# The opening of a four-layer forward pass on one core: constants and vectors issued by SyncE behind the weights, the first weight unit in two transfers, the first piece split ahead of the first squares

## The chip, the cores and the metric

The kernel runs on one core of a Trainium2 chip. The metric is the device time in microseconds of one execution, the median of several. Before the change it is 3043.73 us (three runs, 3043.11 to 3044.73).

## What is computed

Two blocks of two layers each on x of 512 positions by 1024 channels, float32. The first block alternates an even layer (dilated attention beside a short gated convolution) and an odd layer (chunkwise retention), each followed by a gated feed-forward part with a causal depthwise convolution. The second block has two layers of sparse attention (compressed, selected and window branches) beside stick-breaking attention, and the same kind of feed-forward part. Only the beginning of the first layer matters here:

```python
y = xf * lax.rsqrt(jnp.mean(xf * xf, axis=-1, keepdims=True) + EPS)
xn = (y * g.astype(jnp.float32)).astype(x.dtype)
proj = xn @ w_in                        # 1024 -> 1536 + 1536
q, k, v, gate_b, gate_c, h = jnp.split(proj, ...)
q = rms_norm(heads(q), q_gain)
```

## The kernel before, in words

**Layout.** x is held with channels on partitions: eight tiles of 128 channels by 512 positions. The kernel multiplies in float32 by splitting both operands into a rounded high part and the rest: `wh` and `wl` for weights, `xh` and `xl` for activations. Each product of a 128x128 weight column block with a 128x512 tile is three matmuls, wh*xh (L460), wl*xh (L463) and wh*xl (L467).

**Weights.** All weights come in *units* of 128 x 1024 floats (512 KB) into a ring of four slots. A unit has two *pieces* of 512 columns, a piece four blocks of 128. SyncE issues the units in order (`sync_program`, L422); unit u waits until both pieces of unit u-4 have been split. ScalarE makes the high part of each piece (`hi_to`, L973), VectorE the low part (`lo_to`, L1346), and both have four piece buffers: the split of piece i waits until TensorE has used piece i-4. The order is written out by hand: each engine's program says at which points pieces are split, up to three pieces ahead of TensorE.

**The opening.** SyncE issues tile 0 of x and then units 0 to 3. ScalarE issues the eight columns of `vec` that hold the first gains, then the other seven tiles of x in four transfers (L1077), then the rest of `vec`, the constants `cst`, the positions and the mask of the dilated attention (L1079 to L1082), then loads its activation table (L1083). The first norm is taken out of the product: x times the gain goes into TensorE, and the result is later multiplied by the root of the mean square of each position (`rs`). So for each tile j ScalarE makes `xh` (`prescale`, L980) and the square (L984), VectorE `xl` (L1354) and the running sum of squares (L1363). This is `first_tile`. Three output tiles are made at once in the first group: TensorE takes k = 0 to 7 and for each k the next three weight blocks, first the high and low weight of each against `xh(k)`, then the three against `xl(k)`. Piece 0 therefore serves k = 0 and one block of k = 1, piece 1 the rest of k = 1 and two blocks of k = 2.

The driver on ScalarE and VectorE is `group(..., ahead=1)`: `first_tile(0)`, then for each k `first_tile(k + 1)` and the splits up to piece (3(k + 1) - 1) // 4 + 3. On ScalarE the order before is thus: xh0, square 0, xh1, square 1, pieces 0 to 3, xh2, square 2, piece 4 (waits for TensorE), xh3 and so on.

**Who waits for the moved transfers.** The constants are first used by TensorE's column sums of the squares (L557) after the first group, the positions and the rest of `vec` by VectorE well behind that, and the mask by the attention.

**The end of the opening.** Pieces 0 to 5 belong to the first group, 6 and 7 to the next tile, 8 and 9 (unit 4) to the one after it.

Of the kernel before, what the change touches and what calls it, by code (L numbers as in the profile page):

```python
# [16 lines left out]
S = 512  # L17
# [5 lines left out]
RING = 4  # L23
UNIT = 1024
HALF = 512
# [9 lines left out]
NVEC = _at  # L35
# [3 lines left out]
for _name, _n in (("ident", 128), ("ones", 128), ("tri", 128), ("neg", 128), ("rot", 128), ("blk", 2), ("mhalf", 64),  # L39
# [3 lines left out]
NCST = _at  # L43

FLAGS = ("proj", "stat", "attn", "hi", "act", "lo", "dve", "pool", "land0", "land1", "land2", "land3",
         "x0", "x1", "x2", "x3", "x4", "gain", "cst", "vec", "pos", "dil", "ret", "out")


class Flag:
# [329 lines left out]
def build(nc, D, out):  # L379
    with ExitStack() as ctx:  # L380
        K = memory(nc, ctx)
        K.D, K.out, K.W = D, out, weights(D)
        for program in (sync_program, scalar_program, vector_program, gpsimd_program, tensor_program):
            program(Count(), Queue(None), K)
        for flag in K.F:
            flag.count = 0
        block = ctx.enter_context(nc.Block())

        @block.sync
        def _(e):  # L390
            sync_program(e, Queue(e), K)

        @block.scalar
        def _(e):
            scalar_program(e, Queue(e), K)

        @block.vector
        def _(e):
            vector_program(e, Queue(e), K)

        @block.gpsimd
        def _(e):
            gpsimd_program(e, Queue(e), K)

        @block.tensor
        def _(e):
            tensor_program(e, Queue(e), K)


def sync_program(e, q, K):  # L410

    F, W = K.F, K.W
    e.dma_start(K.x(0), K.D["x"][:, 0:S]).then_inc(F.x0.tell("x", by=16), 16)
    for u, (src, width, pieces) in enumerate(W.units):
        if u >= RING:
            before = W.units[u - RING][2]
            for p in before:
                q.wait_ge(F.hi, ("piece", p))
                q.wait_ge(F.lo, ("piece", p))
            if len(before) == 0:  # L420
                q.wait_ge(F.attn, ("unit", u - RING))
        e.dma_start(K.slot(u)[:, 0:width], src).then_inc(K.landed(u).tell(("unit", u), by=16), 16)  # L422
    for j in range(DT):
        if j in (1, 3, 5):
            q.wait_ge(F.pool, ("x", "end", j))
        else:
            q.wait_ge(F.dve, ("x", "end", j))
        e.dma_start(K.out[:, j * S:(j + 1) * S], K.x(j)).then_inc(F.out.tell(("out", j), by=16), 16)
    q.wait_ge(F.out, ("out", DT - 1))
    q.wait_ge(F.proj, ("tile", "down", 3, DT - 1))  # L430
# [529 lines left out]
def scalar_program(e, q, K):  # L960
    F, W, BK = K.F, K.W, K.BK
    nxt = [0]

    def hi_to(p):

        while nxt[0] <= min(p, len(W.pieces) - 1):
            i = nxt[0]
            nxt[0] += 1
            u, c, w = W.pieces[i]
            q.wait_ge(K.landed(u), ("unit", u))  # L970
            if i >= SPLIT:
                q.wait_ge(F.proj, ("piece", i - SPLIT))
            e.activation(K.wh(i, 0, w), K.raw(i), ACT.Copy, bias=0.0, scale=1.0).then_inc(F.hi.tell(("piece", i)), 1)  # L973

    def hi_for(key):
        hi_to(W.ahead(key))

    def prescale(s, j):

        e.activation(K.xh(j), K.x(j), ACT.Copy, bias=0.0, scale=K.vec(GAIN[s][0], GAIN[s][1] + j)).then_inc(  # L980
            F.act.tell(("xh", s, j)), 1)

    def square(s, j, src):
        e.activation(K.tmp(j % 3), src, ACT.Square, bias=0.0, scale=1.0).then_inc(F.act.tell(("sq", s, j)), 1)  # L984
# [5 lines left out]
    def group(key, n, feed, hooks={}, nk=DT, ahead=3):  # L990
        for k in range(ahead):
            feed(k)
        for k in range(nk):
            if ahead == 3:
                hi_to(W.first[key] + ((k + 1) * n - 1) // 4 + 3)
            if k + ahead < DT:
                feed(k + ahead)
            hi_to(W.first[key] + ((k + 1) * n - 1) // 4 + 3)
            if k in hooks:
                hooks[k]()  # L1000
# [66 lines left out]
    def first_tile(j):  # L1067
        q.wait_ge((F.x0, F.x1, F.x2, F.x2, F.x3, F.x3, F.x4, F.x4)[j], "x")
        q.wait_ge(F.gain, "gain")
        if j >= 3:  # L1070
            q.wait_ge(F.dve, ("sqa", s, j - 2))
        prescale(s, j)
        square(s, j, K.x(j))

    e.dma_start(K.VC[:, 0:8], K.D["vec"][:, 0:8]).then_inc(F.gain.tell("gain", by=16), 16)
    for i, (j0, j1) in enumerate(((1, 2), (2, 4), (4, 6), (6, 8))):
        e.dma_start(K.X[:, j0 * S:j1 * S], K.D["x"][:, j0 * S:j1 * S]).then_inc(  # L1077
            (F.x1, F.x2, F.x3, F.x4)[i].tell("x", by=16), 16)
    e.dma_start(K.VC[:, 8:NVEC], K.D["vec"][:, 8:NVEC]).then_inc(F.vec.tell("vec", by=16), 16)  # L1079
    e.dma_start(K.C[:, :], K.D["cst"]).then_inc(F.cst.tell("cst", by=16), 16)  # L1080
    e.dma_start(K.POSI, bass.AP(K.D["pos"].tensor, 0, [[0, 128], [1, S]])).then_inc(F.pos.tell("pos", by=16), 16)
    e.dma_start(K.DIL, K.D["dil"]).then_inc(F.dil.tell("dil", by=16), 16)  # L1082
    e.preload_act_table_set("natural_log_exp_and_others")  # L1083
    group(("e", "g"), 3, first_tile, ahead=1)
    hi_for(("e", 3))
    rs_row(s)
# [150 lines left out]
    for l in range(2):  # L1237
# [47 lines left out]
        for t in range(18):  # L1285
# [31 lines left out]
            if 0 <= t - 2 < 16 and (t - 2) % 4 == 3:  # L1317
                j = (t - 2) // 4
# [16 lines left out]
def vector_program(e, q, K):  # L1335
    F, W, BK = K.F, K.W, K.BK
    nxt = [0]

    def lo_to(p):

        while nxt[0] <= min(p, len(W.pieces) - 1):
            i = nxt[0]
            nxt[0] += 1
            w = W.pieces[i][2]
            q.wait_ge(F.hi, ("piece", i))
            e.tensor_tensor(K.wl(i, 0, w), K.raw(i), K.wh(i, 0, w).bitcast(F32), ALU.subtract).then_inc(  # L1346
                F.lo.tell(("piece", i)), 1)
# [4 lines left out]
    def prescale(s, j):  # L1352
        q.wait_ge(F.act, ("xh", s, j))
        e.scalar_tensor_tensor(out=K.xl(j), in0=K.x(j), scalar=K.vec(GAIN[s][0], GAIN[s][1] + j),  # L1354
                               in1=K.xh(j).bitcast(F32), op0=ALU.mult, op1=ALU.subtract).then_inc(
            F.dve.tell(("xl", s, j)), 1)

    def add_squares(s, j, final):

        q.wait_ge(F.act, ("sq", s, j))  # L1360
        if j > 1:
            q.wait_ge(F.dve, ("sqa", s, j - 1))
        e.tensor_tensor(K.tmp(j % 3), K.tmp(j % 3), K.tmp((j - 1) % 3), ALU.add).then_inc(  # L1363
            F.dve.tell(("sqa", s, j), *([("sq", s)] if j == final else [])), 1)
# [77 lines left out]
    s = ("e",)  # L1442

    def first_tile(j):
        prescale(s, j)
        if j:
            add_squares(s, j, DT - 1)

    def qk_tile(j):
# [3 lines left out]
        times_rs(K.Q[j], key, s, ("qkraw", j))  # L1453

    group(("e", "g"), 3, first_tile, ahead=1)
    late_norm(s, ("e", 3))
    for j in range(3):
# [307 lines left out]
    for l in range(2):  # L1765
# [119 lines left out]
        for t in range(18):  # L1885
            if t < 16:
                j, kt = t // 4, 3 - t % 4
# [295 lines left out]
```

## Time and profile before

| What | us |
|---|---|
| Median of three runs | 3043.73 (3043.11 to 3044.73) |
| The profiled execution's own time | 3045.64 |
| Its span, first to last instruction | 3043.9 |
| TensorE busy in the span | 3007.7 (99%) |
| VectorE busy | 1772.2 (58%) |
| ScalarE busy | 1267.3 (42%) |

The profile is of one execution, its times count from the span's start. PE is TensorE's matmuls, PEld its weight loads, DVE VectorE, ACT ScalarE, SP SyncE; a name with a q at the end (SPq, ACTq) is the engine's own issuing of DMAs. A matmul's duration in the timeline is longer than the distance to the next one, since matmuls overlap; in the chain in order of time each stands with the part in which it was the last. The granted clock of TensorE is given as a share of 2.4 GHz: 1.00 or 0.50.

### The profile page before, as it was taken

The numbers are of one execution on the slowest core, as the hardware profiler recorded it, in microseconds if no ns is written. First come the engines' busy times: TensorE is split into PE (matmuls) and PEld (weight loads), VectorE is DVE, ScalarE is ACT, GpSimd is POOL, SyncE is SP. The second block draws the span as 40 slices with busy tenths as digits, with TensorE's granted clock in tenths as the row PEclk, the third lists the DMA queues.
The fourth block names the chain that finished last, engine by engine and source line by source line (L and its number), as shares of the span: only waits on it lengthen the run. The fifth ranks groups of instructions, "written<-read, shape, count | busy, mean of one in ns | idle before, by whom it ended". The sixth has DMA issues, their size and how long they took to land.

```text
span 3043.9 us, 37845 instructions
## 1 busy us (share of the span) xinstructions
PE 3007.7 (99%) x14656; PEld 2403.0 (79%) x14656; DVE 1772.2 (58%) x3123; ACT 1267.3 (42%) x2374; POOL 146.3 (5%) x203
## 2 busy tenths in 40 slices
PE   8999999999999999999999999999999999999998
PEld 7678888888778888888866687888788766788886
DVE  4565875345554487634465567775364655577743
ACT  4344443323223344432366544443233655354431
POOL 0100000000000000001001101000020011010000
PEclk9899999999999999999999999999999999999999
DMA  3222323222222233332311132323232011223332
GB/s 143 75 87 95 100 97 97 97 89 76 82 78 84 90 104 97 97 97 92 102 38 42 42 98 81 100 97 97 90 99 91 29 49 46 93 84 104 97 97 69
DMA packets 71891, 260.35 MB, mean 86 GB/s; under 512 B 8096, under 2 KB 8096, under 8 KB 71584
## 3 DMA queue, kind: packets, MB, share of 16 engines
q1 hardware_dynamic: 70272, 252.67, 25.9%
q10 hardware_dynamic: 1440, 5.26, 0.4%
q8 instruction: 116, 1.90, 0.3%
q14 instruction: 63, 0.52, 0.1%
HBM read 255.81 MB, written 2.10 MB: 85 GB/s over the span
## 4 chain that ended last, share of the span: by engine, by line
PE 93%; DVE 4%; ACT 2%; issue 1%; ACTq 0%; POOL 0%; DVEq 0%
PE bank L460 25%; PE bank L463 24%; PE bank L467 24%; PE bank L537 2%; PE bank L541 2%; PE bank L538 2%; PE bank L617 2%; PE bank L649 2%; PE bank L631 1%; PE bank L773 1%; PE bank L890 1%; DVE wl L1346 1%; DVE big L1919 1%; PE bank L920 1%; ACT big L1325 1%
## 5 line engine op out<-in xcount | busy, mean ns | idle before, releaser
L1346 DVE TENSOR_TENSOR wl<-ring,wh 128x512 fp32r<-128x512 f32 (+1 forms) x944 | 646.8, 691 | 820.9 <-ACT wh L973 815.8
L460 PE MATMUL bank<-xh,wh 128*128 128x512 f32 x2464 | 989.0, 401 | 17.7 <-ACT wh L973 10.7
L463 PE MATMUL bank<-xh,wl 128*128 128x512 f32 x2464 | 966.9, 392 | 0.4 <-DVE wl L1346 0.3
L467 PE MATMUL bank<-xl,wh 128*128 128x512 f32 x2464 | 926.5, 391 | 0.0
L973 ACT ACTIVATE wh<-ring 128x512 fp32r<-128x512 f32 (+1 forms) x944 | 579.4, 622 | 810.5 <-PE bank L467 732.2
L460 PEld LDWEIGHTS bank<-xh,wh 128*128 128x128 f32 x2464 | 466.5, 189 | 152.8 <-issue 38.3
L467 PEld LDWEIGHTS bank<-xl,wh 128*128 128x128 f32 x2464 | 465.2, 189 | 99.7 <-DVE xl L1439 0.4
L463 PEld LDWEIGHTS bank<-xh,wl 128*128 128x128 f32 x2464 | 467.0, 190 | 92.0 <-DVE wl L1346 1.6
L460 PE MATMUL bank<-bigr,wh 128*128 128x512 f32 x1024 | 399.1, 390 | 0.6 <-ACT bigr L1329 0.6
L463 PE MATMUL bank<-bigr,wl 128*128 128x512 f32 x1024 | 398.5, 389 | 0.0
L467 PE MATMUL bank<-bigr,wh 128*128 128x512 f32 x1024 | 393.5, 389 | 0.0
L460 PEld LDWEIGHTS bank<-bigr,wh 128*128 128x128 f32 x1024 | 192.2, 188 | 41.4 <-ACT bigr L1329 1.4
L467 PEld LDWEIGHTS bank<-bigr,wh 128*128 128x128 f32 x1024 | 192.2, 188 | 40.6 <-DVE bigr L1923 0.9
L463 PEld LDWEIGHTS bank<-bigr,wl 128*128 128x128 f32 x1024 | 192.3, 188 | 39.6
L1142 ACT ACTIVATE tmp<-tmp,vec 128x512 f32<-128x512 f32 x136 | 104.7, 770 | 182.0 <-DVE tmp L1396 182.0
L1042 ACT ACTIVATE pp<-pp,sm 128x512 f32<-128x512 f32 (+3 forms) x160 | 88.3, 553 | 91.3 <-DVE sm L1415 91.1
L1152 ACT ACTIVATE bigr<-tmp 128x512 fp32r<-128x512 f32 x88 | 55.6, 632 | 138.3 <-DVE tmp L1591 138.3
L1396 DVE TENSOR_TENSOR big<-bank,rs 128x512 f32<-128x512 f32 x106 | 71.6, 687 | 69.1 <-PE bank L467 66.0
L1948 POOL TENSOR_TENSOR sm<-sm,cst 128x4 f32<-128x4 f32 x16 | 16.6, 1036 | 1952.6 <-DVE sm L1368 1618.5
L1396 DVE TENSOR_TENSOR tmp<-bank,rs 128x512 f32<-128x512 f32 x154 | 105.3, 684 | 6.9 <-ACT rs L988 4.3
L537 PE MATMUL bank<-wh,xh 128*128 128x512 f32 (+1 forms) x288 | 106.8, 371 | 0.0
L541 PE MATMUL bank<-wl,xh 128*128 128x512 f32 (+1 forms) x288 | 105.8, 367 | 0.0
(199 smaller groups left out, 2766.6 us busy)
## 6 DMA issues: line engine op xcount, KB each, us to landing
ring<-in_w_up SPq DMA_DIRECT2D x176, 512.0 KB, 3.4
ring<-in_w_down SPq DMA_DIRECT2D x88, 512.0 KB, 3.4
ring<-in_w_in SPq DMA_DIRECT2D x64, 512.0 KB, 3.5
ring<-in_w_ret SPq DMA_DIRECT2D x32, 512.0 KB, 3.2
ring<-in_w_even SPq DMA_DIRECT2D x20, 512.0 KB, 3.5
ring<-in_w_ret_v SPq DMA_DIRECT2D x16, 512.0 KB, 3.3
ring<-in_w_ret_out SPq DMA_DIRECT2D x16, 512.0 KB, 3.3
ring<-in_w_proj SPq DMA_DIRECT2D x16, 512.0 KB, 3.4
```

What stands on the lines that cost most here:

```text
L460: e.matmul(o, K.wh(p, c * 128, 128), oh, start=start, stop=False, skip_group_check=True)
L463: e.matmul(o, K.wl(p, c * 128, 128), oh, start=False, stop=False, skip_group_check=True)
L467: m = e.matmul(o, K.wh(p, c * 128, 128), ol, start=False, stop=stop, skip_group_check=True)
L537: e.matmul(o, K.XH[:, c], K.wh(p, 0, n), start=k == 0, stop=False)
L538: e.matmul(o, K.XL[:, c], K.wh(p, 0, n), start=False, stop=False)
L541: m = e.matmul(o, K.XH[:, c], K.wl(p, 0, n), start=False, stop=k == DT - 1)
L617: m = e.matmul(BK[i][:, u.at:u.at + w], u.q[r, u.qt * 128:w], u.k[r, 0:w], start=True, stop=True, skip_group_check=True)
L973: e.activation(K.wh(i, 0, w), K.raw(i), ACT.Copy, bias=0.0, scale=1.0).then_inc(F.hi.tell(("piece", i)), 1)
L1042: e.activation(p, p, ACT.Exp, bias=K.den(t, 2 * part + i, 0), scale=-1.0, accum_out=K.den(t, 2 * part + i, 1)).then_inc(F.act.tell(("exp", ...
L1142: e.activation(K.tmp((2 * i + 1) % 5), K.up(i), ACT.Identity, bias=b, scale=w[2]).then_inc(F.act.tell(("tap", f, i)), 1)
L1346: e.tensor_tensor(K.wl(i, 0, w), K.raw(i), K.wh(i, 0, w).bitcast(F32), ALU.subtract).then_inc(F.lo.tell(("piece", i)), 1)
L1396: e.tensor_tensor(dst, K.bank(key)[:, :], K.RSB[:, :], ALU.mult).then_inc(F.dve.tell(("freed", *key), *events), 1)
```

## The change

Three edits, all in the opening.

1. The four transfers of the rest of `vec`, `cst`, the positions and the mask leave ScalarE's program. SyncE issues them, right after unit 3 and ahead of unit 4.
2. Unit 0 comes in two transfers of 128 x 512 floats. The first tells a flag of its own, `first`, for which ScalarE's split of piece 0 waits; the second tells the unit's flag, for which piece 1 waits.
3. In `first_tile(0)` ScalarE splits piece 0 (high part) between xh0 and the square of tile 0, and VectorE splits it (low part) ahead of xl0.

```diff
--- before.py
+++ after.py
@@ -43,7 +43,7 @@
 NCST = _at
 
 FLAGS = ("proj", "stat", "attn", "hi", "act", "lo", "dve", "pool", "land0", "land1", "land2", "land3",
-         "x0", "x1", "x2", "x3", "x4", "gain", "cst", "vec", "pos", "dil", "ret", "out")
+         "x0", "first", "x1", "x2", "x3", "x4", "gain", "cst", "vec", "pos", "dil", "ret", "out")
 
 
 class Flag:
@@ -419,7 +419,16 @@
                 q.wait_ge(F.lo, ("piece", p))
             if len(before) == 0:
                 q.wait_ge(F.attn, ("unit", u - RING))
-        e.dma_start(K.slot(u)[:, 0:width], src).then_inc(K.landed(u).tell(("unit", u), by=16), 16)
+        if u == 0:
+            e.dma_start(K.slot(u)[:, 0:HALF], src[:, 0:HALF]).then_inc(F.first.tell("first", by=16), 16)
+            e.dma_start(K.slot(u)[:, HALF:width], src[:, HALF:width]).then_inc(K.landed(u).tell(("unit", u), by=16), 16)
+        else:
+            e.dma_start(K.slot(u)[:, 0:width], src).then_inc(K.landed(u).tell(("unit", u), by=16), 16)
+        if u == RING - 1:
+            e.dma_start(K.VC[:, 8:NVEC], K.D["vec"][:, 8:NVEC]).then_inc(F.vec.tell("vec", by=16), 16)
+            e.dma_start(K.C[:, :], K.D["cst"]).then_inc(F.cst.tell("cst", by=16), 16)
+            e.dma_start(K.POSI, bass.AP(K.D["pos"].tensor, 0, [[0, 128], [1, S]])).then_inc(F.pos.tell("pos", by=16), 16)
+            e.dma_start(K.DIL, K.D["dil"]).then_inc(F.dil.tell("dil", by=16), 16)
     for j in range(DT):
         if j in (1, 3, 5):
             q.wait_ge(F.pool, ("x", "end", j))
@@ -967,7 +976,10 @@
             i = nxt[0]
             nxt[0] += 1
             u, c, w = W.pieces[i]
-            q.wait_ge(K.landed(u), ("unit", u))
+            if i == 0:
+                q.wait_ge(F.first, "first")
+            else:
+                q.wait_ge(K.landed(u), ("unit", u))
             if i >= SPLIT:
                 q.wait_ge(F.proj, ("piece", i - SPLIT))
             e.activation(K.wh(i, 0, w), K.raw(i), ACT.Copy, bias=0.0, scale=1.0).then_inc(F.hi.tell(("piece", i)), 1)
@@ -1070,16 +1082,14 @@
         if j >= 3:
             q.wait_ge(F.dve, ("sqa", s, j - 2))
         prescale(s, j)
+        if j == 0:
+            hi_to(0)
         square(s, j, K.x(j))
 
     e.dma_start(K.VC[:, 0:8], K.D["vec"][:, 0:8]).then_inc(F.gain.tell("gain", by=16), 16)
     for i, (j0, j1) in enumerate(((1, 2), (2, 4), (4, 6), (6, 8))):
         e.dma_start(K.X[:, j0 * S:j1 * S], K.D["x"][:, j0 * S:j1 * S]).then_inc(
             (F.x1, F.x2, F.x3, F.x4)[i].tell("x", by=16), 16)
-    e.dma_start(K.VC[:, 8:NVEC], K.D["vec"][:, 8:NVEC]).then_inc(F.vec.tell("vec", by=16), 16)
-    e.dma_start(K.C[:, :], K.D["cst"]).then_inc(F.cst.tell("cst", by=16), 16)
-    e.dma_start(K.POSI, bass.AP(K.D["pos"].tensor, 0, [[0, 128], [1, S]])).then_inc(F.pos.tell("pos", by=16), 16)
-    e.dma_start(K.DIL, K.D["dil"]).then_inc(F.dil.tell("dil", by=16), 16)
     e.preload_act_table_set("natural_log_exp_and_others")
     group(("e", "g"), 3, first_tile, ahead=1)
     hi_for(("e", 3))
@@ -1442,6 +1452,8 @@
     s = ("e",)
 
     def first_tile(j):
+        if j == 0:
+            lo_to(0)
         prescale(s, j)
         if j:
             add_squares(s, j, DT - 1)
```

## Rows read from the trace of the kernel before

**Rows 1.** The page: TensorE's busy share, and the chain's share by engine.
```profile
PE 3007.7 (99%) x14656; PEld 2403.0 (79%) x14656; DVE 1772.2 (58%) x3123; ACT 1267.3 (42%) x2374; POOL 146.3 (5%) x203
...
PE 93%; DVE 4%; ACT 2%; issue 1%; ACTq 0%; POOL 0%; DVEq 0%
```

**Rows 2.** Timeline from 0 us, queues and ScalarE: start us, length us, engine, line.
```profile
0.80 0.39 SPq L413 DMA_DIRECT2D x<-in_x  x1
1.25 2.37 ACTq L1077 DMA_DIRECT2D x<-in_x  x4
...
1.72 1.62 SPq L422 DMA_DIRECT2D ring<-in_w_even  x3
...
3.65 0.49 ACTq L1079 DMA_DIRECT2D vec<-in_vec  x1
...
5.74 1.28 ACT L1083 ACT_TABLE_LOAD   x1 [5.74 <-issue]
7.04 0.72 ACT L980 ACTIVATE xh<-x,vec 128x512 fp32r<-128x512 f32 x1
7.67 0.61 ACT L984 ACTIVATE tmp<-x 128x512 f32<-128x512 f32 x1
...
9.32 2.17 ACT L973 ACTIVATE wh<-ring 128x512 fp32r<-128x512 f32 x4
```

**Rows 3.** The same timeline: TensorE's first matmuls and VectorE's first low splits.
```profile
10.08 0.76 PE L460 MATMUL bank<-xh,wh 128*128 128x512 f32 x1 [10.08 <-ACT wh L973]
10.20 2.49 DVE L1346 TENSOR_TENSOR wl<-ring,wh 128x512 fp32r<-128x512 f32 x4
...
10.94 0.80 PE L463 MATMUL bank<-xh,wl 128*128 128x512 f32 x1
...
14.52 0.63 PE L460 MATMUL bank<-xh,wh 128*128 128x512 f32 x1
...
17.48 0.39 PE L460 MATMUL bank<-xh,wh 128*128 128x512 f32 x1
```

**Rows 4.** DMA issues one by one, KB, us to landing; then the window 20.50:21.00.
```profile
x<-in_x SPq DMA_DIRECT2D x1, 256.0 KB, 3.4
vec<-in_vec ACTq DMA_DIRECT2D x1, 4.0 KB, 3.6
...
ring<-in_w_even SPq DMA_DIRECT2D x1, 512.0 KB, 4.8
x<-in_x ACTq DMA_DIRECT2D x1, 256.0 KB, 5.1
...
ring<-in_w_even SPq DMA_DIRECT2D x1, 512.0 KB, 6.9
x<-in_x ACTq DMA_DIRECT2D x1, 512.0 KB, 7.4
...
x<-in_x ACTq DMA_DIRECT2D x1, 512.0 KB, 11.2
...
20.50:21.00 0.50, 0.50 (x4) 0.42 (x3) 0.50 (x2) 0.50 (x2) 0.00 (x0) 1.00 0.01 4
```

In the last of these rows the columns are the window, its length, busy time of PE, PEld, DVE, ACT and POOL with their instructions, TensorE's granted clock, the DMA engines' share and GB/s.

**Rows 5.** The chain in order of time (start, us, what); then the window 40.50:41.00.
```profile
13.44 1.28 PE bank L467 x3
...
16.43 0.32 PE bank L460
...
43.15 0.43 PE bank L463
...
40.50:41.00 0.50, 0.50 (x3) 0.40 (x2) 0.46 (x1) 0.00 (x0) 0.00 (x0) 0.50 0.00 0
```

**Rows 6.** Timeline: unit 4's issue, piece 8's split, and the first column sums.
```profile
11.57 0.33 SPq L422 DMA_DIRECT2D ring<-in_w_even  x1
...
27.72 0.63 ACT L973 ACTIVATE wh<-ring 128x512 fp32r<-128x512 f32 x1 [0.56 <-PE bank L467]
...
31.77 0.95 PE L557 MATMUL bank<-cst,tmp 128*128 128x1 f32 x8
```

## The prediction

> **What bounds the kernel now.** The first thing to read is the share of busy time and the chain that ended last. The reader is to see that TensorE is busy 99% of the span and that 93% of the chain is matmuls [rows 1]. So nothing shortens this kernel except fewer or faster matmuls, or a TensorE that starts earlier or waits less. The change adds and removes no matmul. It touches the first microseconds alone, so the second view is the timeline of ScalarE and the two issuing queues before TensorE's first matmul [rows 2]. ScalarE's own stream is one line: it issues the DMAs of the gain vector and of four stretches of x, then four more (vectors, constants, positions, mask) from 3.65 us, and only at 5.74 us loads its table. Then come xh0 at 7.04, the square of tile 0 at 7.67, xh1 with its square and, at 9.32, the first split of a weight piece. The first matmul starts at 10.08 and the second, which needs the low half of the piece, at 10.94 [rows 3]. Before that TensorE does nothing, and from 10.94 on it never stands in the first group. ScalarE and VectorE then wait for it, not it for them. So the question is how much earlier 10.94 comes, and whether the stretch behind it follows.
>
> **The change, part by part.**
>
> **Four issues leave ScalarE.** They fill 3.65 to 5.74 [rows 2], so the table load and all of ScalarE behind it move by 2.09 us: xh0 from 7.04 to 4.95. Its inputs allow it: x0 was issued at 0.80 [rows 2] and took 3.4, the gains were issued beside it and took 3.6, so both are there by 4.4 [rows 4]. Gain 2.09.
>
> **Piece 0 is split straight behind xh0.** Before, its split began 2.28 us after xh0 began (9.32 less 7.04), behind two squares and xh1. Now it begins one instruction later, 0.63 (7.67 less 7.04). Gain 1.65, and the split starts at 5.58.
>
> **Its data.** The whole first unit of 512 KB was issued at 1.25 and took 4.8 [rows 4], which is 6.05: with only that flag the split would start 0.47 late. The first half alone is not in this trace. The bounds are 4.65 (1.25 plus the 3.4 of the 256 KB of x0, the least loaded transfer) and 6.05 (no earlier than the whole). The nearest row in size and issue time is x1, 256 KB issued at 1.25 and landed after 5.1, but that one stands behind the gains in ScalarE's queue, while the half stands first behind x0 and its own other half can't be ahead of it. I take 5.58 or sooner, cost 0, and keep 0 to 0.47. The second half, one issue later, is wanted by piece 1 only near 8.1, two microseconds after the whole unit's 6.05.
>
> **VectorE splits the low half first.** Before, the first high half was done at 9.86 (9.32 and a quarter of the 2.17 of four), but VectorE was still adding squares, and the low split began at 10.20 [rows 3], 0.34 later. Now VectorE has nothing ahead of it. Between 0 and 0.34, I take 0.3. xl0 comes after the low split, which lasts about 0.65 (a quarter of 2.49 is 0.62), so from 7.0 to about 7.7. Its first user is the seventh matmul, five matmuls of 0.43 behind the second, near 9.1. It costs nothing.
>
> **Sum.** 2.09 + 1.65 + 0.3 = 4.0, less 0.1 of hand-overs that I leave room for, 3.9 us: the second matmul moves from 10.94 to 7.0.
>
> **Does the rest follow?** With ScalarE as above: split 5.58, square 6.2, xh1 6.8 (x1 landed at 6.35), square 7.5, then pieces 1, 2, 3. Unit 1 was issued at 1.72 and took 6.9, so it is there at 8.6; SyncE now issues one more transfer ahead of it, 0.47, at most 9.1. So the splits end near 10.2 and xh2 runs from 10.2 to 10.9 (x2 landed at 1.72 + 7.4 = 9.1) [rows 4]. TensorE's second step starts at 14.52 less 3.9 = 10.6 and its third at 17.48 less 3.9 = 13.6 [rows 3], so both have what they need. The last stretch of x was issued before 3.1 and took 11.2, so it landed by 14.3, and its first user, xh6, comes five microseconds later at the least (after the unit splits of four more steps of 2 us). No load becomes the bound.
>
> **The moved transfers.** On SyncE they cost four issues of about half a microsecond, 2 us ending near 6. The next thing in its program, unit 4, waits for the low half of piece 1 anyway and was issued at 11.57 [rows 6], so nobody waits for these 2 us. In the queues the same bytes move. All that was issued in the first 13 us had been moved by 20.5, where the rate falls to 4 GB/s [rows 4], and last in line means about that, or 21 with the hand-over. The constants' first user is the sums at 31.77 [rows 6], 27.9 afterwards: seven microseconds of cover. Unit 4 has less. Its first piece is split at 27.72, or 23.8 afterwards, and now the vectors, constants, positions and mask stand ahead of it in its own queue. Cover 2.8 us, cost 0. If that cover went, the split of piece 8 would be late first and TensorE after it.
>
> The Trainium skill (DMA: Bandwidth & Descriptors, Issuing engines are not separate DMA queues) says that transfers issued from different engines run on the same 16 DMA engines and interleave, and that a second issuing engine saves only issue time. By it the move is worth the issue time alone and nothing in bandwidth, as in the sum. The same page (Queues, rings and completion order) says that descriptors of one ring are consumed in its order, which speaks against the change: this is the rival of unit 4 below.
>
> **The clock.** TensorE's level is best read from the matmuls: in the chain in order of time three of them take 1.28 us at 13.44, 0.43 each, and at 16.43 one takes 0.32, between the levels [rows 5]; in the timeline one lasts 0.63 at 14.52 and 0.39 at 17.48 [rows 3]. 0.43 is the lower level, 1.2 GHz: the same 0.43 stands at 43.15, at the end of a stretch in which the granted clock is 0.50. (The windows of the first 16 us say 1.00, which these durations contradict.) So TensorE ran at half speed from its start to about 16.5, 6.4 us after its first matmul. If the rise again comes that long after the start, it moves with it and the gain is whole. If it came at the same instant as before, the 3.9 us won would hold half-speed work only and be worth 1.95. I take the first, since what the engine does is what has moved.
>
> **Predicted time.** The profiled execution took 3045.64 us, span 3043.9 and 1.7 around it; it is 1.9 above the median of 3043.73. It would become 3041.7. The gain is a shift of the start, so I take the same 3.9 off the median: 3039.8, or 0.13%. About 0.2% (6.1 us) is what a measurement of this kernel can tell from no change, so this counts as the same.
>
> **Rivals.**
> 1. *The clock does not follow.* Gain 1.95, 3041.8. For it: the clock was low again around 40.5 to 43.6 without TensorE being idle for long [rows 5], so its instants aren't tied to one matmul. Against it: the rise at 16.5 follows a steady run of matmuls. Chance 0.12.
> 2. *The half unit lands no sooner than the whole, or ScalarE's table load does not move up fully.* The first alone leaves 3.4, 3040.3; with half of the 2.09 lost as well, 2.4, 3041.3. For it: ScalarE's four x issues and SyncE's share the time from 1.25 to 3.6, and SyncE now issues more in it. Chance 0.10.
> 3. *Unit 4 stands behind the constants.* This ends slower. Place: the split of piece 8, wanted at 23.8. Every microsecond of landing beyond that is one of TensorE. A landing at 27.7 eats the whole gain, 3043.7, and one at 33.9 makes the kernel slower by over 0.2%, 3049.8. Against it: the bytes need no longer than until 21, and the delay would have to be 7 to 13 us on top. The page's rule on ring order, above, gives the order and not this delay. Chance 0.03.
> 4. *Half-speed stretches further on fall otherwise.* The one around 40.5 to 43.6 cost half of its 3.1 to 3.6, or 1.7. Were it gone, the gain would be 5.6, 3038.1; over 6.1 needs another such stretch gone too, 3036.4. Or one comes on top, and the gain is 2.2. Chance 0.10, of which 0.04 is beyond 0.2%.
>
> The forecast itself has 0.65. **The range** goes from 3037.3 (rival 4's 3038.1 less 0.8 for the spread of runs, which is 1.6 from lowest to highest) to 3043.0 (rival 1's 3041.8, with 0.5 of landing and 0.7 of spread). Chances: faster by over 0.2% 0.04, slower by over 0.2% 0.03, within it 0.93.
>
> **What the profile after would show.** The table load at 3.65; xh0 near 4.95; the first weight split near 5.6; the first matmul near 6.3 and the second near 7.0; matmuls without a gap from there; their time in the chain falling from 0.43 each near 12.6; the sums of the first norm near 27.9; unit 4 landed before 24. A first matmul at 8 or later, a wait of TensorE for a split within the first 30 us, or a rise of the clock at 16.5 would prove a step wrong.

## The result, and the profile after

The changed kernel takes 3039.61 us (median of 12 runs, 3035.62 to 3043.24) against 3043.2 of the kernel before (12 runs, 3041.79 to 3047.55). The ratio is 0.9984, with a 95% interval of 0.9976 to 0.9992 (the quotient of the two medians alone is 0.9988). That is 3.6 us of medians where 3.9 was forecast, within the range and within 0.2%. The interval lies below 1, so the gain is clear of noise, but it stands for 2.4 to 7.3 us, and 3.6 can't be told from 3.9 nor from 5.

The profiled executions differ by more: 3045.64 before and 3038.69 after, 7.0 us. So the second question is where the other three come from. First the opening, in the timeline of the changed kernel: start, length, engine, line, what it does, and in brackets the idle time before it. These lines answer to [rows 2, 3].

```profile
1.25 0.42 SPq L423 DMA_DIRECT2D ring<-in_w_even  x1
1.25 2.30 ACTq L1091 DMA_DIRECT2D x<-in_x  x4
1.72 0.42 SPq L424 DMA_DIRECT2D ring<-in_w_even  x1
2.18 1.59 SPq L426 DMA_DIRECT2D ring<-in_w_even  x3
3.58 1.28 ACT L1093 ACT_TABLE_LOAD   x1 [3.58 <-issue]
3.81 0.71 SPq L428 DMA_DIRECT2D vec<-in_vec  x1
...
4.87 0.72 ACT L992 ACTIVATE xh<-x,vec 128x512 fp32r<-128x512 f32 x1
...
5.50 0.61 ACT L985 ACTIVATE wh<-ring 128x512 fp32r<-128x512 f32 x1
...
6.14 0.69 DVE L1356 TENSOR_TENSOR wl<-ring,wh 128x512 fp32r<-128x512 f32 x1 [6.14 <-ACT wh L985]
...
6.26 0.77 PE L469 MATMUL bank<-xh,wh 128*128 128x512 f32 x1 [6.26 <-ACT wh L985]
...
6.89 0.79 PE L472 MATMUL bank<-xh,wl 128*128 128x512 f32 x1
...
7.48 0.63 PE L469 MATMUL bank<-xh,wh 128*128 128x512 f32 x1
...
7.91 0.63 PE L472 MATMUL bank<-xh,wl 128*128 128x512 f32 x1
...
8.13 0.63 ACT L985 ACTIVATE wh<-ring 128x512 fp32r<-128x512 f32 x1 [0.36 <-DMA ring<-in_w_even]
...
10.01 0.39 PE L469 MATMUL bank<-xh,wh 128*128 128x512 f32 x1
...
10.23 0.39 PE L472 MATMUL bank<-xh,wl 128*128 128x512 f32 x1
...
10.66 1.15 ACT L985 ACTIVATE wh<-ring 128x512 fp32r<-128x512 f32 x2 [1.90 <-DMA ring<-in_w_even]
...
11.37 0.84 PE L476 MATMUL bank<-xl,wh 128*128 128x512 f32 x3
11.72 0.71 ACT L992 ACTIVATE xh<-x,vec 128x512 fp32r<-128x512 f32 x1
...
12.48 0.50 PE L469 MATMUL bank<-xh,wh 128*128 128x512 f32 x1 [0.27 <-ACT xh L992]
```

The reader is to see three things. The table load has moved from 5.74 to 3.58, and everything up to the second matmul follows, from 10.94 to 6.89. ScalarE now stands for data, which it did not before: 1.90 us until 10.66, for unit 1. And xh2, behind the two pieces of that unit in ScalarE's program, is late: TensorE's last three matmuls of the second step begin at 11.37, the next would have followed near 12.05 and comes at 12.48. That is a new wait of 0.4 us.

Next the chain in order of time (start, length, what), first the column sums of the first norm and then the 24 short matmuls that follow it. Before:

```profile
31.93 0.79 PE bank L557 x8
...
37.38 2.84 PE bank L584 x24
```

And after:

```profile
27.07 0.79 PE bank L566 x8
...
32.52 2.84 PE bank L593 x24
```

So the opening as a whole is 4.86 us shorter: 4.05 until the second matmul, less about 0.5 for the new wait, and the rest because the half-speed clock ended sooner. In the timeline the distance between matmuls falls from 0.43 to 0.23 near 9.5, 3.2 us behind the first matmul, where before it fell near 16.5, 6.4 us behind it. From the second matmul on that is 3.0 us less at half speed, worth 1.5. Behind this point, the windows show TensorE's granted clock. The columns are the window, its length, the busy times of PE, PEld, DVE, ACT and POOL, the clock, the DMA share and GB/s. Before:

```profile
36.00:46.00 10.00, 9.94 (x49) 8.16 (x48) 4.33 (x7) 3.60 (x6) 0.00 (x0) 0.83 0.15 52
88.00:114.00 26.00, 25.94 (x61) 13.40 (x61) 9.77 (x16) 7.66 (x14) 0.00 (x0) 0.67 0.14 48
1818.00:1842.00 24.00, 20.34 (x93) 16.83 (x92) 15.39 (x23) 9.32 (x16) 4.34 (x3) 0.86 0.14 44
```

And after:

```profile
36.00:46.00 10.00, 10.00 (x49) 8.40 (x48) 2.81 (x5) 2.42 (x4) 0.00 (x0) 1.00 0.30 86
88.00:114.00 26.00, 25.94 (x80) 14.71 (x80) 16.33 (x34) 7.72 (x18) 0.00 (x0) 0.80 0.23 81
1818.00:1842.00 24.00, 20.33 (x85) 16.77 (x84) 18.95 (x25) 10.28 (x18) 8.20 (x6) 0.79 0.16 56
```

The half-speed stretch near 40 us is gone and the one near 92 is shorter, 2 x 0.20 x 26 = 10.4 us instead of 2 x 0.33 x 26 = 17.2, while the one near 1825 is longer, and so is the one near 2200 (10.2 us instead of 6.8). In sum 41.0 us at half speed instead of 44.4, worth 1.7. So of the 7.0 us of this pair 4.9 lie in the opening, 1.7 in the clock further on, and 0.4 are left. The question for the runs is which of that belongs to the change.

### The profile page after: what moved, and what is told of

Its sections match the earlier page's. It is cut to its first block, busy times and chain, and to the rows that moved or that the text cites. A ratio compares the mean times of both kernels' runs of the same rounds, so it can differ in the third digit from the quotient of the medians.

```text
span 3036.9 us, 37846 instructions
## 1 busy us (share of the span) xinstructions
PE 3004.3 (99%) x14656; PEld 2400.7 (79%) x14656; DVE 1773.7 (58%) x3123; ACT 1267.4 (42%) x2374; POOL 146.0 (5%) x203
## 4 chain that ended last, share of the span: by engine, by line
PE 93%; DVE 4%; ACT 2%; issue 1%; DMA 0%; POOL 0%; SPq 0%; DVEq 0%
PE bank L469 25%; PE bank L472 24%; PE bank L476 24%; PE bank L546 2%; PE bank L550 2%; PE bank L547 2%; PE bank L626 2%; PE bank L658 2%; PE bank L640 1%; PE bank L782 1%; PE bank L899 1%; DVE wl L1356 1%; DVE big L1931 1%; PE bank L929 1%; PE bank L581 1%
```

## The experiments

### The two halves of the change

`moved_only` leaves unit 0 whole and piece 0 in its old place. Like all that follow, its edit is shown against the changed kernel, and in part:

```diff
-        if u == 0:
-            e.dma_start(K.slot(u)[:, 0:HALF], src[:, 0:HALF]).then_inc(F.first.tell("first", by=16), 16)
...
-        if j == 0:
-            hi_to(0)
...
-        if j == 0:
-            lo_to(0)
```

> Only the first edit: the four transfers go from ScalarE to SyncE; unit 0 stays whole and piece 0 is split in the old place. By the prediction's sum the table load starts near 3.6, ScalarE moves up 2.1, and the second matmul comes at 10.94 - 2.1 = 8.8; the time falls by 2.1 us, to a ratio of 0.9993. Unit 1 lands at 8.6 as before, so TensorE does not wait later. Rival (the start is shared with the clock's instant): the start moves by 2.1, the time by about 1 only.

Measured: 3042.99 us, ratio 0.9998 (0.9989 to 1.0007). The table load came at 3.62 as expected, but the second matmul only at 9.41, 1.5 earlier than before and not 2.1. The timeline shows what took the rest:

```profile
6.65 0.72 ACT L985 ACTIVATE xh<-x,vec 128x512 fp32r<-128x512 f32 x1 [0.49 <-DMA x<-in_x]
```

ScalarE reached xh1 before tile 1 of x had landed. Before, the four issues hid this. Part of what they cost had been free, since the data behind them were not there yet. Unit 1 landed at 9.0 (8.6 expected), TensorE did not wait, and the 24 short matmuls began at 34.42, 3.0 earlier than before. The median is 0.65 us lower with an interval of about 2.7 to either side, so it tells the expected 2.1 neither from 1 nor from nothing.

`early_only` keeps the four transfers on ScalarE:

```diff
-        if u == RING - 1:
-            e.dma_start(K.VC[:, 8:NVEC], K.D["vec"][:, 8:NVEC]).then_inc(F.vec.tell("vec", by=16), 16)
...
+    e.dma_start(K.VC[:, 8:NVEC], K.D["vec"][:, 8:NVEC]).then_inc(F.vec.tell("vec", by=16), 16)
...
     e.preload_act_table_set("natural_log_exp_and_others")
```

> Only the second and third edits: unit 0 in halves and piece 0 split ahead of the squares; the four transfers stay with ScalarE, so its table load stays at 5.74. The sum gives 1.65 + 0.3 = 1.9: second matmul near 9.0, ratio 0.9994. Theory of turns (the two queues give their descriptors in turn, and a half unit has as many as a whole one): unit 1 lands near 10.6 as in the changed kernel, 2 us later than before. Theory of bytes: unit 1 lands by 9.1. Either way ScalarE gets to piece 2 near 10.1 to 10.7, so no wait of TensorE near 12 is expected, or one below 0.2.

Measured: 3041.37 us, 0.9994 (0.9986 to 1.0003). Second matmul at 9.48, 1.5 earlier, and not the 9.0 expected: the four issues took longer and the table was loaded at 6.17. Unit 1 landed at 2.18 + 8.3 = 10.5, as the theory of turns has it. TensorE did not wait behind its start, as both had it.

The two parts win 1.5 each alone and 4.1 together in the best case. Both stand in ScalarE's one stream, so by the sum they add, 2.1 and 1.9. Each alone fell short for a reason of its own: the first waited 0.5 for tile 1 of x, and in the second the table load came 0.4 later than before. Together the first loss is gone, since the split of piece 0 runs ahead of xh1, which then starts at 6.54, behind the landing of tile 1 at 5.6. In the medians these parts can't be told apart, since the intervals are 2.7 us to either side.

### Why unit 1 came late

`whole_unit` is the changed kernel without the two transfers; piece 0 waits for the unit's flag again:

```diff
-            e.dma_start(K.slot(u)[:, 0:HALF], src[:, 0:HALF]).then_inc(F.first.tell("first", by=16), 16)
...
+        e.dma_start(K.slot(u)[:, 0:width], src).then_inc(K.landed(u).tell(("unit", u), by=16), 16)
```

> The changed kernel with unit 0 in one transfer again. Piece 0 then waits for the whole unit, near 5.6 to 6.05 where the changed kernel splits at 5.50, so the second matmul comes near 7.3 (0 to 0.5 later than 6.89). Theory of turns: unit 1 lands near 8.6 instead of 10.6, ScalarE does not stand 1.9 us ahead of piece 2, xh2 is early and TensorE's wait at 12.05 to 12.48 is gone: what is lost at the start (0.4) comes back (0.4), and the time is within 0.3 us of the changed kernel's. Theory of bytes: unit 1 lands as late as in the changed kernel, the wait stays, and the kernel is 0.4 slower than the changed one.

Measured: 3039.73 us, 0.9989 (0.9980 to 0.9998). Unit 0 landed late, at 6.95, so the second matmul came at 8.40, outside what was expected. Unit 1 landed at 9.2, as the theory of turns has it. TensorE did not wait near 12, but that decides nothing: two later profiles of the changed kernel have no wait there either (below). The time is the same as the changed kernel's in the next set of runs (3039.75, `after_again`), so no run shows that the two transfers of unit 0 are worth anything in the median.

`quarters` makes the effect larger, with four transfers in place of the two:

```diff
-            e.dma_start(K.slot(u)[:, 0:HALF], src[:, 0:HALF]).then_inc(F.first.tell("first", by=16), 16)
-            e.dma_start(K.slot(u)[:, HALF:width], src[:, HALF:width]).then_inc(K.landed(u).tell(("unit", u), by=16), 16)
+            e.dma_start(K.slot(u)[:, 0:256], src[:, 0:256]).then_inc(F.first.tell("quarter", by=16), 16)
+            e.dma_start(K.slot(u)[:, 256:512], src[:, 256:512]).then_inc(F.first.tell("first", by=16), 16)
+            e.dma_start(K.slot(u)[:, 512:768], src[:, 512:768]).then_inc(K.landed(u).tell("quarter", by=16), 16)
+            e.dma_start(K.slot(u)[:, 768:width], src[:, 768:width]).then_inc(K.landed(u).tell(("unit", u), by=16), 16)
```

> The changed kernel with unit 0 in four transfers of 128 x 256 floats. Same bytes, four times the descriptors of the whole unit. Theory of turns: each quarter lands with the x transfer beside it, so quarters 2, 3 and 4 land at about 8, 10.5 and 13, piece 0 can be split near 7 to 8 only, unit 1 lands past 13, and TensorE waits for pieces 1 and 2 for several us. Theory of bytes: the first half lands near 5.5 as in the changed kernel and unit 1 near 10.6, no new wait but for the issue time of two more transfers (0.9).

Measured, in one execution (3039.03 us): unit 1 landed at 3.2 + 8.8 = 12.0. With unit 0 whole it landed between 8.6 and 9.2 (four profiles), with two halves by columns between 10.0 and 10.9 (five profiles). The quarters landed at 4.9, 6.6, 8.8 and 10.5, sooner than the 8, 10.5 and 13 that I had written: I had given each turn the time of two full transfers, though a quarter's turn moves 128 KB beside x's 512. TensorE did not wait for pieces 1 and 2, where I had expected several us. The direct evidence stands in the queues' own lines of this run, in the stretch from 5 to 7 us (q10 is ScalarE's queue, with x; q1 SyncE's, with the weights; packets, MB, share of 16 engines).

```profile
q10 hardware_dynamic: 153, 0.56, 80.2%
q1 hardware_dynamic: 146, 0.13, 20.2%
```

As many packets each, but a quarter of the bytes in q1, whose packets are 1 KB against 4 KB. In the changed kernel, in the same stretch, q1 had 131 packets with 0.28 MB and q10 118 with 0.46. So the two queues share by packets and not by bytes, and a transfer cut along its columns has as many packets in each part as the whole: it gives the other queue twice the bytes while it passes. Beside the 0.46 us of the later issue, that is the delay of unit 1.

`row_halves` was to tell turns by packet from turns by transfer:

```diff
-            e.dma_start(K.slot(u)[:, 0:HALF], src[:, 0:HALF]).then_inc(F.first.tell("first", by=16), 16)
-            e.dma_start(K.slot(u)[:, HALF:width], src[:, HALF:width]).then_inc(K.landed(u).tell(("unit", u), by=16), 16)
+            e.dma_start(K.slot(u)[0:64, 0:width], src[0:64]).then_inc(F.first.tell("rows", by=16), 16)
+            e.dma_start(K.slot(u)[64:128, 0:width], src[64:128]).then_inc(F.first.tell("first", by=16), 16)
...
-            if i == 0:
+            if u == 0:
                 q.wait_ge(F.first, "first")
```

> The changed kernel with unit 0 in two transfers of 64 rows x 1024 floats instead of 128 rows x 512; piece 0 and piece 1 both wait for both. As many transfers as in the changed kernel, but as many rows in all as in a whole unit. If the queues take turns by rows (descriptors), unit 1 lands as after a whole unit, at 8.6 to 9.2 (issued at 2.18, to landing 6.5 to 7.0). If they take turns by transfers, or if the extra issue is what delays it, unit 1 lands as in the changed kernel, at 10.1 to 10.9 (to landing 8.3 to 8.7). The second matmul comes at 7.4 to 8.4, since piece 0 needs the whole unit.

Measured, in one execution (3042.86 us): neither. Unit 1 landed at 2.48 + 10.4 = 12.9, unit 0 at 10.45, and the second matmul came at 11.91. The windows of this kernel show another effect that covers the question:

```profile
7.00:8.00 1.00, 0.00 (x0) 0.00 (x0) 0.00 (x0) 0.00 (x0) 0.00 (x0) 1.00 1.06 258
```

The DMA engines are busy all the time (share 1.06) but move 258 GB/s, where the kernel before moved 430 in the same window. From 5 to 10 us, while the two transfers of 64 rows were under way beside x's, it was 221 to 283 GB/s in four of the five windows of 1 us and 385 in the other; why, no run here shows. The packet counts are not equal here either (from 5 to 7 us q1 had 37 and q10 133). So this run does not separate turns by packet from turns by transfer, and equal counts are shown only for transfers of 128 rows.

### The new wait, and a start without the x issues

`x_first` makes tile 2 behind piece 1, on both engines (ScalarE's part is shown):

```diff
-            if k + ahead < DT:
+            if k + ahead < DT and not (ahead == 1 and k == 1):
                 feed(k + ahead)
+            if ahead == 1 and k == 0:
+                hi_to(1)
+                feed(2)
```

> The changed kernel, with tile 2 of x (xh2, its square, xl2) made behind piece 1 and ahead of pieces 2 and 3, on ScalarE and VectorE. My theory: TensorE's wait of 0.4 us at 12.05 to 12.48 comes from xh2 standing behind pieces 2 and 3, which wait for unit 1 until 10.66. With xh2 ready near 9.4 the third step starts at 12.05 and everything behind is 0.4 earlier: 0.4 us less than the changed kernel in the chain, no less than 3039.2 in the median and hardly to be told from it there. Rival: the third step then waits for piece 2 instead (split at 10.66, low half 11.33 to 12.0, wanted near 13), and nothing is won.

Measured: 3040.72 us, 0.9989 (0.9980 to 0.9998), not to be told from the changed kernel. In its timeline the third step follows the second without a gap:

```profile
11.49 0.84 PE L476 MATMUL bank<-xl,wh 128*128 128x512 f32 x3
12.17 0.39 PE L469 MATMUL bank<-xh,wh 128*128 128x512 f32 x1
```

Though its second matmul came at 7.01, 0.12 later than in the first profile of the changed kernel, its 24 short matmuls began at 32.06, 0.46 earlier. No wait for piece 2 came in its place. But this profile does not prove that the new order removed the wait. Unit 1 landed at 10.05 here, not at 10.65, and with the old order the two pieces and xh2 behind them (1.15 and 0.72 us) would have been done near 11.95, ahead of 12.17. The changed kernel itself has no gap in its third profile, where unit 1 landed at 10.04:

```profile
11.79 0.84 PE L476 MATMUL bank<-xl,wh 128*128 128x512 f32 x3
12.47 0.39 PE L469 MATMUL bank<-xh,wh 128*128 128x512 f32 x1
```

Nor has it one in `after_again`. There unit 1 landed later, at 10.86, but TensorE had started 1.3 us later as well. What does show the cause is the first profile: xh2 ended at 12.43, behind the two pieces that had waited for unit 1, and the third step began at 12.48 with xh2 as the releaser. The wait came in one of three profiles, where the second matmul was early, the half-speed clock short and unit 1 late all at once.

`one_queue` takes three of the four x issues from ScalarE as well:

```diff
+        if u < 3:
+            e.dma_start(K.X[:, (2 + 2 * u) * S:(4 + 2 * u) * S], K.D["x"][:, (2 + 2 * u) * S:(4 + 2 * u) * S]).then_inc(
+                (F.x2, F.x3, F.x4)[u].tell("x", by=16), 16)
...
+    e.dma_start(K.x(1), K.D["x"][:, S:2 * S]).then_inc(F.x1.tell("x", by=16), 16)
```

> x_first with three of ScalarE's four x transfers issued by SyncE between the units (x0, unit 0 in halves, x tiles 2-3, unit 1, tiles 4-5, unit 2, tiles 6-7, unit 3, constants); ScalarE issues the gains and tile 1 and loads its table at 1.7 instead of 3.6. Theory of the sum: the issues on ScalarE bound the start, until data does: xh0 starts when the gains land, near 4.2, piece 0 is split when its half lands, near 4.9, second matmul near 6.3, 0.6 earlier than in the changed kernel. Unit 1 lands near 8 to 8.6, since no queue takes turns any more. Rival: the load of the halves is the bound already and the second matmul stays at 6.8 or later. Median 3038.6 by the theory, 3039.6 by the rival.

Measured: 3040.77 us, 0.9990 (0.9982 to 0.9999). The table was loaded at 1.73, yet the second matmul came at 6.83. The line of xh0 says why:

```profile
4.67 0.72 ACT L995 ACTIVATE xh<-x,vec 128x512 fp32r<-128x512 f32 x1 [1.66 <-DMA vec<-in_vec]
```

The gains, 4 KB issued at 0.81, are there at 4.6, and the half unit at 5.4, when xh0 is done. The rival is right: after the change the data bound the start, and nothing is left in ScalarE's issues. Unit 1 landed at 9.5 where 8 to 8.6 was expected.

### The price of a ring's order

`consts_first` moves the four transfers ahead of three units, for the prediction's third rival:

```diff
-        if u == RING - 1:
+        if u == 0:
             e.dma_start(K.VC[:, 8:NVEC], K.D["vec"][:, 8:NVEC]).then_inc(F.vec.tell("vec", by=16), 16)
```

> The changed kernel with the four moved transfers issued right behind unit 0, ahead of units 1 to 3. It prices the third rival of the prediction (a queue gives its transfers in ring order). By it unit 1 lands only behind their 1.8 MB, near 16 instead of 10.7, ScalarE and with it xh2 stand until then, TensorE waits from 12.0 to about 18 and the kernel is some 6 us slower than the changed one: about 3045.5, ratio 1.0006 or more, if the clock falls besides another 1 to 2. If the queue did not hold to its order, unit 1 would land near 11 to 12 and the time stay within 1 us of the changed kernel's.

Measured: 3049.64 us, 1.0017 (1.0008 to 1.0026), 9.9 above the changed kernel of the same set. Unit 1 landed at 4.47 + 12.4 = 16.9, and TensorE's third step waited for it:

```profile
13.23 0.86 PE L476 MATMUL bank<-xl,wh 128*128 128x512 f32 x3
18.75 0.80 PE L469 MATMUL bank<-xh,wh 128*128 128x512 f32 x1 [4.66 <-ACT xh L992]
```

The queue holds to its order: the four transfers landed at 10.6, 13.7, 15.0 and 15.7, and unit 1 behind them. The Trainium skill has it so (DMA: Bandwidth & Descriptors, Queues, rings and completion order: descriptors of a ring are consumed in ring order), and the trace agrees with these landings. The wait is about 4.8 us, and the granted clock fell to 0.50 from 16 to 23 us. Until the 24 short matmuls the kernel is 7.3 to 8.5 us behind the changed one's three profiles, and 9.9 in the median, more than the 6 to 8 expected. The mechanism of the rival exists, then. In the change itself it has cover.

### Both kernels once more

No edit.

> The changed kernel itself, on the chip and beside the runs of this set, as the measure for the other three: 3039.6, ratio 0.9988. A second profile of it also tells what in the first one was chance: the second matmul should be within 0.2 us of 6.89 and the wait near 12 be there again, while the instant at which the clock rises (9.6 there) and the half-speed stretches near 40 and 91 may differ.

> The kernel before once more, for its spread from execution to execution. ScalarE bounds its start, so the second matmul should come at 10.94 within 0.3, wherever the data land; the sums of the first norm within 1.5 of 31.93, the difference coming from how long the half-speed clock lasts behind the first matmul (6.3 us in the first profile, 3 to 6 in the others).

> The changed kernel a third time. Its start is bound by the landing of the first half, which came at 5.45 and 6.75 in two executions, and by ScalarE, which is ready at 5.4 to 5.5. So the second matmul should come between 6.9 and 8.2, 1.4 us behind the later of the two, and unit 1 land at 10.1 to 10.9 in any case.

Measured: 3039.75 us for `after_again`, ratio 0.9988 (0.9979 to 0.9997), the first result again. The single execution of `before_look` took 3045.79 and that of `after_look` 3043.30. These two and `row_halves` ran on another chip than the rest. In `after_again` the second matmul came at 8.18 and not within 0.2 of 6.89, for the half unit landed at 6.75, and the wait near 12 that was expected again was not there. In `after_look` the second matmul came at 6.83, the half landing at 5.35, and unit 1 landed at 10.04, both just ahead of what was expected. In the other kernels with halves by columns the half landed between 5.4 and 5.9. Before, the second matmul came at 10.94 and 10.99: ScalarE bound that start, and the data's scatter did not show. The half-speed clock behind the first matmul (until the distance between matmuls falls from 0.43 to 0.23) lasted 6.4 and 6.5 us in the two profiles of before, 3.2, 3.8 and 4.2 in the three of the changed kernel, and between 3.1 and 6.3 in the other kernels. The expectation on the sums before, 32.08 measured, holds.

### All profiles in one sum

For each profile I take the span, less the instant at which the 24 short matmuls begin, less half of the time at half speed behind it (twice one minus the granted clock, summed over windows of 1 us, the last 20 us left out).

| Kernel | span | 24 matmuls begin | half-speed time behind | rest |
|---|---|---|---|---|
| before | 3043.9 | 37.38 | 44.4 | 2984.3 |
| before_look | 3044.1 | 37.53 | 44.4 | 2984.4 |
| after | 3036.9 | 32.52 | 41.0 | 2983.9 |
| after_again | 3038.9 | 33.53 | 41.0 | 2984.9 |
| after_look | 3041.6 | 32.37 | 51.2 | 2983.6 |
| moved_only | 3036.0 | 34.42 | 34.1 | 2984.5 |
| early_only | 3038.6 | 35.61 | 37.6 | 2984.2 |
| whole_unit | 3038.5 | 33.44 | 41.0 | 2984.6 |
| x_first | 3037.1 | 32.06 | 40.9 | 2984.6 |
| consts_first | 3044.1 | 40.86 | 37.4 | 2984.5 |

(`quarters` and `row_halves` give 2984.3 and `one_queue` 2983.6.) The rest is the same within 1.3 us, whatever the kernel, while the opening moves by 8.8 us. Before, the 24 matmuls begin at 37.4 and 37.5, in the changed kernel at 32.4 to 33.5, so the opening is 3.9 to 5.2 us shorter. A microsecond won at the start is a microsecond of the whole, nothing gives it back later, and what scatters from one execution to the next is the time at half speed: 34 to 51 us, worth up to 8.6. `after_look` shows it best. It has nearly the shortest opening and is still only 2.3 us faster than before.

## Why the prediction was right, point by point

**Four issues off ScalarE, 2.09.** Right, 2.16: the table load came at 3.58. `moved_only` shows that alone it would not all have arrived, since x1 was not there.

**Piece 0 one instruction behind xh0, 1.65.** Right: 0.63 from 4.87 to 5.50.

**The half unit lands in time, cost 0 to 0.47.** Right in two of three profiles with hardly a margin (in the first it landed at 5.4, and the split began at 5.50), and wrong in its bound: I held 6.05 for the latest, because the whole unit had landed then, but one execution in three had it at 6.75. The landing of a whole unit scatters too (6.05 to 6.95). A bound taken from one trace is not a bound. This costs 0 to 1.3 us from execution to execution. Whether it is why the median gain of 3.6 is under 3.9 no run shows: the interval (2.4 to 7.3) is far wider than the difference.

**VectorE's low half at once, 0.3.** Right: it starts 0.03 behind the split.

**Sum 3.9.** Second matmul forecast at 7.0, measured at 6.89, 8.18 and 6.83. That the medians come within 0.3 us of it is in part luck. The opening won 1.0 to 1.5 us that the sum did not have, since behind the second matmul the half-speed clock lasted 2.0 to 3.1 us less in the three profiles than before, and it lost up to 1.3 to the late half and up to 0.5 to the wait for xh2.

**"No load becomes the bound."** Wrong by 0.4 us in one of three profiles. The step that failed is that unit 1 would be late by one issue, 0.47, and there at 9.1 at most. It was issued 0.46 later and landed at 10.65, 10.86 and 10.04, where a whole unit 0 had it at 8.6 to 9.2, because each half of unit 0 takes as many packets as the whole. And since ScalarE's program has xh2 behind the pieces of unit 1, TensorE's third step, which needs little of unit 1, can wait for all of it. It did so in the first profile; in the other two xh2 was ready 1.0 and 0.6 us before it was wanted. The 9.1 was also a bound taken from one trace: with unit 0 whole, unit 1 landed anywhere from 8.6 to 9.2.

**The moved transfers, cost 0.** Right. Unit 4 was issued at 9.58 and took 10.8, so it landed at 20.4 (forecast 21), and the split of piece 8 waited only for TensorE:

```profile
22.86 0.63 ACT L985 ACTIVATE wh<-ring 128x512 fp32r<-128x512 f32 x1 [0.56 <-PE bank L476]
```

**The clock.** Its rise was forecast near 12.6, as long after the first matmul as before. Wrong in the profile: the matmuls were fast from 9.5 on, after 3.2 us. The rival of the same instant (16.5) is as wrong. Over the profiles the delay lies between 3.1 and 6.5 us, so neither rule holds for one execution. For the median it came out near the whole gain, which 12 runs with a spread of 7.6 us can't prove within a microsecond.

**Rivals.** The late half (second) happened in one of three profiles. Ring order (third) is real and costs 9.9 us where it has no cover. The half-speed stretch near 40 us (fourth) did vanish in the profiled execution, as it did in four others (`moved_only`, `whole_unit`, `after_again`, `x_first`), and it was there in both profiles of before, in `early_only`, `quarters`, `row_halves` and `consts_first` and, longer, in `after_look` and `one_queue`. The record shows what goes with it: in the five profiles without this stretch the half-speed clock behind the first matmul had lasted 3.8 us or less, in the eight with it 4.2 or more. Since the same changed kernel has both kinds, it varies from execution to execution; whether the change makes the short kind more frequent, two profiles of before can't tell. The gain of 7.0 in the first pair of profiles was thus 4.9 of opening, of which over 1 came by the clock, and 1.7 of clock further on.

## What to carry to other kernels

When one engine issues DMAs, loads its table and computes, its issues delay its first result one for one, but only until the data land: look for the landing first, and expect that, once the engine is ready sooner, the next microsecond belongs to the transfers. In front of the first matmul, order each engine's program by what TensorE needs next and not by unit, so that a late load holds back only what needs it; here that was worth 0.4 us in one of three profiles and could not be seen in the median. If a change is worth a few microseconds, sum it at a landmark behind the opening, and check the clock before believing the difference of two spans.

## What the runs showed of the hardware

Two queues that were both full moved about as many packets each and not as many bytes: 153 packets with 0.56 MB against 146 with 0.13 MB in the same 2 us. A transfer with shorter rows got less of the bandwidth, and splitting one by columns delayed what stood behind it (unit 1 at 8.6 to 9.2, 10.0 to 10.9 and 12.0 for one, two and four parts, of which 0.5 us for each added part is its issue). With transfers of 64 rows the counts were unequal, 37 against 133.

While 256 KB transfers into 64 of the 128 partitions were under way, the DMA engines were busy (share 1.06) at 258 GB/s, against 430 in the same window of the kernel before.

A DMA of 4 KB takes 3.2 to 3.9 us from issue to landing at the start of the kernel, no less than the one of 256 KB issued beside it (3.1 to 3.7).

TensorE's half-speed clock lasted from 3.1 to 6.5 us behind the first matmul, and the sum of its later half-speed stretches varied from 34 to 51 us between executions. In the three profiles of the changed kernel these stretches make 5.1 us of difference (41.0 to 51.2, halved), and the opening 1.2.
